# Two-layer hybrid decoder trunk: at the three layer ends, who normalises the first tokens, and where TensorE turns them

## The reference, cut to what matters

```
mod = (cs @ ada_w[l] + ada_b[l])[:, None, :]
sh_a, sc_a, g_a, sh_m, sc_m, g_m = jnp.split(mod, N_MOD, axis=-1)
x = layer_norm(DEEPNORM_ALPHA * x + (1.0 + g_a) * y, ln_g[l, 0], ln_b[l, 0])
h = x * (1.0 + sc_m) + sh_m
```

## Time and profile before

| what | value |
|---|---|
| median of three runs (lowest to highest) | 2274.39 us (2272.28 to 2275.78) |
| span of the profiled execution | 2271.9 us |
| TensorE busy | 2237.7 us, 98% |
| VectorE busy | 1722.1 us, 76% |
| ScalarE busy | 1142.2 us, 50% |
| mean granted TensorE clock | 0.998 of full |

### The profile page before, as it was taken

The page is one execution under the profiler, slowest core; times in us unless marked ns, Lnnn a source line. Parts: engine busy times, 40 slices in busy tenths (PEclk is TensorE's granted clock), DMA queues, the critical chain, the costliest instruction groups (busy, mean ns, idle before and its releaser), DMA issues.

```text
span 2271.9 us, 31928 instructions
## 1 busy us (share of the span) xinstructions
PE 2237.7 (98%) x10980; PEld 1882.2 (83%) x10980; DVE 1722.1 (76%) x1697; ACT 1142.2 (50%) x1420; POOL 19.0 (1%) x41
## 2 busy tenths in 40 slices
PE   7999999999999999999999999999999999999998
PEld 6887788788888888888888888888888888888886
DVE  6689788988888888898777867788766445556656
ACT  2144365565555554444555555555555555444443
POOL 1000000000000000000000000000000000000000
PEclk9999999999999999999999999999999999999999
DMA  9998899679999999969758766884877555755553
GB/s 393 417 371 328 343 390 385 219 287 370 378 372 378 374 371 347 342 241 356 284 218 324 271 237 233 317 311 135 310 286 264 188 187 201 255 192 193 194 206 127
DMA packets 146475, 658.61 MB, mean 290 GB/s; under 512 B 16496, under 2 KB 16816, under 8 KB 115792
## 3 DMA queue, kind: packets, MB, share of 16 engines
q1 hardware_dynamic: 144000, 642.05, 75.9%
q0 software_dynamic: 2384, 15.37, 1.7%
HBM read 655.22 MB, written 2.13 MB: 289 GB/s over the span
## 4 chain that ended last, share of the span: by engine, by line
PE 80%; DMA 9%; DVE 6%; issue 3%; ACT 2%; SPq 1%; DVEq 0%; ACTq 0%
PE ps L1421 19%; PE ps L1320 15%; PE ps L1324 15%; PE ps L1321 15%; PE ps L1425 10%; DMA mod_w<-in_mods 3%; DMA R<-in_mods 3%; DMA raw<-in_tiles 2%; DVE mod_w L880 2%; DVE w_lo L875 2%; ACT w_hi L436 1%; PE ps L1577 0%; PE ps L1523 0%; PE ps L1521 0%; PE ps L1522 0%
## 5 line engine op out<-in xcount | busy, mean ns | idle before, releaser
L875 DVE TENSOR_TENSOR w_lo<-raw,w_hi 128x1024 fp32r<-128x1024 f32 x720 | 877.4, 1223 | 451.1 <-ACT w_hi L436 447.2
L436 ACT ACTIVATE w_hi<-raw 128x1024 fp32r<-128x1024 f32 x720 | 760.3, 1059 | 837.0 <-PE ps L1324 374.9
L1320 PE MATMUL ps<-w_hi,h_both 128*128 128x512 f32 x1872 | 735.5, 393 | 2.3 <-ACT w_hi L436 2.3
L1321 PE MATMUL ps<-w_hi,h_both 128*128 128x512 f32 x1872 | 729.1, 389 | 0.0
L1324 PE MATMUL ps<-w_lo,h_both 128*128 128x512 f32 x1872 | 506.9, 390 | 2.8 <-DVE w_lo L875 2.6
L1421 PE MATMUL ps<-h_both,w_hi 128*128 128x512 f32 x1920 | 480.9, 392 | 0.0
L880 DVE SCALAR_TENSOR_TENSOR mod_w<-mod_w,cs 128x2048 f32<-128x2048 f32 x200 | 457.0, 2286 | 30.0 <-DMA mod_w<-in_mods 22.4
L1324 PEld LDWEIGHTS ps<-w_lo,h_both 128*128 128x128 f32 x1872 | 350.7, 188 | 79.7 <-DVE w_lo L875 6.6
L1320 PEld LDWEIGHTS ps<-w_hi,h_both 128*128 128x128 f32 x1872 | 351.6, 188 | 77.5 <-ACT w_hi L436 2.7
L1321 PEld LDWEIGHTS ps<-w_hi,h_both 128*128 128x128 f32 x1872 | 351.6, 188 | 72.3 <-issue 1.0
L1421 PEld LDWEIGHTS ps<-h_both,w_hi 128*128 128x128 f32 x1920 | 345.4, 189 | 61.8
(11 more groups left out here) (196 smaller groups left out, 1045.9 us busy)
## 6 DMA issues: line engine op xcount, KB each, us to landing
raw<-in_tiles SPq DMA_DIRECT2D x736, 512.0 KB, 4.8
mod_w<-in_mods SPq DMA_DIRECT2D x200, 1024.0 KB, 7.1
R<-in_mods SPq DMA_DIRECT2D x16, 1024.0 KB, 21.9
odd_raw<-in_tiles SPq DMA_DIRECT2D x16, 512.0 KB, 20.5
R<-in_tiles SPq DMA_DIRECT2D x16, 512.0 KB, 6.6
R<-in_ln_rows POOLq DMA_DIRECT2D x6, 1024.0 KB, 8.5
G<-in_mods SPq DMA_DIRECT2D x4, 1024.0 KB, 21.9
S<-in_mods SPq DMA_DIRECT2D x4, 1024.0 KB, 23.9
```

The lines of the kernel that those rows point to most:

```text
L436: nc.scalar.activation(w_hi[:, slot, :], raw[:, slot, :], ACT.Copy).then_inc(hi_ready, 1)
L875: nc.vector.tensor_tensor(w_lo[:, slot, :], raw[:, slot, :], w_hi[:, slot, :].bitcast(F32), ALU.subtract)\
L1320: mm(dst, h_hi[:, kt, toks], w_hi[:, slot, c], start=start, stop=False, skip_group_check=more)
L1321: return mm(dst, h_lo[:, kt, toks], w_hi[:, slot, c], start=False, stop=False, skip_group_check=more)
```

## The change

Three edits, at all three ends. **VectorE** now normalises columns 0 to 1023 of token group 0, with the instruction that L969 uses elsewhere, twice 512 columns. This stands inside the third part (token group 1, first block), between its multiply (L955) and its add (L956), and waits for the variance and for ScalarE's exponential. **ScalarE** loses the two tiny instructions and the two of 512 columns; the rest of its list, the quoted loop included, stays. **TensorE** loses the eight transposes of the identity, and makes the transposes of pairs 0 and 1 before the last of the 14 entries, not behind it; pairs 2 and 3 stay at the head of `early_tiles`.

```diff
-WARM = 8
             def layer_end(e, occ_n, occ, n_coef, co):
                 scale_of(occ_n, 0)
-                act.wait_ge(rstd_ready, 2 * occ_n + 1)
-                link(nc.scalar.activation(ssq[:, 0:1], rstd[:, 0:1], ACT.Copy, scale=-1.0))
-                link(nc.scalar.activation(ssq[:, 1:2], mv[:, 0, 0:1], ACT.Identity, scale=ssq[:, 0:1]))
-                for q in range(2):
-                    x = X[:, 0, q * SW:(q + 1) * SW]
-                    nc.scalar.activation(x, x, ACT.Identity, scale=rstd[:, 0:1], bias=ssq[:, 1:2]).then_inc(xn0_ready, 1)
                 act.wait_ge(coef_ready, n_coef)
...
-            def residual(occ, half, tok, alpha, ns=(0, 1), parts=LAST_PARTS):
+            def residual(occ, half, tok, alpha, ns=(0, 1), parts=LAST_PARTS, between=None):
...
                 link(nc.vector.tensor_tensor(stage, ps[:, bank:bank + len(ns), :].rearrange("p a n -> p (a n)"), G[:, cols], ALU.mult))
+                if between is not None:
+                    between()
                 link(nc.vector.scalar_tensor_tensor(X[:, tok, cols], X[:, tok, cols], alpha, stage, ALU.mult, ALU.add))
...
-            def last_parts(occ, alpha):
+            def last_parts(e, occ, alpha):
+                def first_columns():
+                    dve.wait_ge(var_ready, 2 * occ + 1)
+                    dve.wait_ge(rstd_ready, 2 * occ + 1)
+                    for q in range(2):
+                        x = X[:, 0, q * SW:(q + 1) * SW]
+                        nc.vector.tensor_scalar(x, x, mv[:, 0, 0:1], rstd[:, 0:1], ALU.subtract, ALU.mult).then_inc(xn0_ready, 1)
+
                 for tok, ns in LAST_PARTS:
-                    link(residual(occ, 1, tok, alpha, ns))
+                    link(residual(occ, 1, tok, alpha, ns, between=first_columns if (tok, ns) == LAST_PARTS[2] else None))
...
-                for pr in range(EARLY):
+                for pr in range(EARLY // 2, EARLY):
                     turn_token(occ, e, pr, 0)
...
-            def wide(t, half, first, src, hooks=None, last=False, down=False):
+            def wide(t, half, first, src, hooks=None, next_stage=None, down=False):
+                last = next_stage is not None
...
-                    for i in range(WARM):
-                        nc.tensor.transpose(ps[:, 1 if down else 5, (i % 4) * P:(i % 4 + 1) * P], ident[:], ident[:])
+                        if i == len(LAST_TILES) - 2:
+                            for pr in range(EARLY // 2):
+                                turn_token(*next_stage, pr, 0)
...
-            wide(O + 16, 1, True, narrow, last=True)
+            wide(O + 16, 1, True, narrow, next_stage=(H_M0, 0))
...
-                        wide(t + 3 * BODY, half, False, src(3), {}, last=True, down=True)
+                        wide(t + 3 * BODY, half, False, src(3), {}, next_stage=(H_Q, 1), down=True)
...
-            wide(O + 16, 1, True, heads, last=True)
+            wide(O + 16, 1, True, heads, next_stage=(H_M1, 2))
```

More of the change, by code:

```diff
@@ L986, in layer_end @@
             def layer_end(e, occ_n, alpha, occ, n_coef, co):
-                last_parts(occ_n, alpha)
+                last_parts(e, occ_n, alpha)
                 for q in range(2):
```

## The result

The changed kernel takes 2277.57 us (median of 21 runs, 2275.49 to 2281.78), the kernel before 2274.08 us (median of 21 runs, 2272.16 to 2276.31). The ratio is 1.0017, with a 95% interval of 1.0011 to 1.0022: slower by 3.5 us by the medians, inside the 0.2% that was called no change. 2276.7 was forecast. The span of the profiled execution is 2274.2 us against 2271.9, and the execution itself took 2275.9 us.

What follows compares the result with a forecast made beforehand. TensorE, busy 98% of the span, was taken as the bound, so longer layer ends reach the time in full. Delays of 0.74 + 0.79 + 0.78 = 2.31 us on 2274.39 gave 2276.7 us, range 2272.8 to 2280.0.

Steps and rivals of the forecast that it cites:

- TensorE busy in every microsecond between the ends: Windows behind the layer ends: TensorE never idle (682.00 of 682.00 us behind the first), so an end's delay counts in full.
- VectorE's add 1.02 us later: VectorE's third part at the first end: two normalisations push the add from 439.64 to 440.66, 1.02 us later.
- The release by the exponential: VectorE's third part: the normalisations start 0.11 us after ScalarE's exponential ends, at 439.73.
- the fourth part's slack: VectorE's fourth part: its waits for TensorE, 0.28, 0.23 and 0.24 us at the ends, absorb delay first.
- Idle transposes worth nothing: TensorE at each end: dropping eight idle transposes saves it 0.87 us, none of which reaches the time.
- the 1.33 us of head start: TensorE at the first end: with_hi can begin at 441.97 instead of 443.30, but none of this gain arrives.
- What is late next: ScalarE's pair 2 waits for token group 1's variance; TensorE stands still from 443.85 to about 445.9, two microseconds.
- The clock: At the layer ends, TensorE's clock falls in the two-microsecond stall: 1.7 us an end, 5.0 in all, 2281.7 us; 7%.

Runs made afterwards that it cites:

- vec_only: The changed kernel with TensorE's list of the kernel before (eight idle transposes kept, all four pairs turned behind the last entry); 2276.52 us, ratio 1.0009 to the kernel before.
- vec_double: The changed kernel with two more VectorE normalisations of 512 columns behind the new ones, into a free buffer nobody reads; 2281.56 us.
- no_idle: The kernel before without the eight idle transposes, nothing else changed; 2273.67 us, ratio 0.9999 to the kernel before.
- scale_late: The changed kernel with ScalarE's scale of token group 1 moved behind all four pairs' copies and the first h_lo copy; 2271.35 us, ratio 0.9994 to the kernel before.
- fill_transposes: The changed kernel with 16 identity transposes in TensorE's wait between the products of pairs 1 and 2; 2276.03 us.
- fill_products: The changed kernel with 8 unused products of 512 columns in TensorE's wait between the products of pairs 1 and 2; 2276.05 us.

## Why the prediction was right, and where it fell short

- **TensorE busy in every microsecond between the ends, so all of an end reaches the time:** it has no wait there after the change either. Held.
- **VectorE's add 1.02 us later:** measured 1.70 - 0.66 = 1.04. The release by the exponential took 0.14 us where 0.11 was taken.
- **Less the fourth part's slack, 0.74, 0.79 and 0.78 us for the ends, 2.31 in all:** the ends are 0.78, 0.80 and 0.78 longer, 2.36. vec_only gives the same length, and vec_double adds 0.92 for two more normalisations.
- **Idle transposes worth nothing, the 1.33 us of head start lost again:** no_idle changes an end by 0.03 us; the head start was 1.50 less 0.15 by which the entries came earlier, 1.35, and all of it went into the wait.
- **What is late next:** ScalarE's pair 2 behind the scale of token group 1, TensorE idle for two microseconds. It is 1.9 us, three times. scale_late removes it by that order alone.
- **The clock:** here the text fell short. It weighed the fall as a case of its own, at 7%, that either takes the ends or not, and its reason against it was that the kernel before has only transposes and a short wait from 441.09 to 443.30 at a clock of 1.00. The reason was sound for a stretch with transposes in it, as fill_transposes shows, and was carried over to one without. In truth the fall comes in some executions, at one end or another, about half of the runs having a mean clock that speaks for one. The price was near: 1.7 us a fall was taken, 1.48 measured (1.3 and 1.1 in vec_double). So the mechanism was right for 2.4 of the 3.5 us. The other 1.1 us were in no term of the sum. The clock, set to nothing there, should have had one; that it makes up the whole 1.1 is an estimate from medians and not shown.

## What to carry to other kernels

Ask for each wait in an engine's list what is queued behind it that does not need it: here the scale of the second half's tokens stood in front of copies that were ready, and moving that one call was worth more (1.5 us an end) than all the work that the change took off TensorE and ScalarE. Work that is taken off the busiest engine brings nothing where another chain ends last, and an engine's slack (0.28 us ahead of the fourth part) is used up before a cost shows, so read it first. And where TensorE is left idle for about two microseconds between products, count the chance of a slower clock behind it too, and look at more than one profile for it.

## What the runs showed that was not expected

- The same kernel, with the same wait of 1.9 us, has its clock at 1.00 behind it in five of the six ends that were profiled, and a mean of 0.57 over the next window in one. With 2.8 us it fell in two of three.
- The fall at the program's start, which gave the prediction its price, is not bound to the first long wait either: in fill_products' profile TensorE waited 3.87 us up to 16.07 and the clock was 1.00 from 16 to 20 us; it fell later, behind a wait of 2.10 us that ended at 44.64 (0.61 from 44 to 48 us).
- Filling the wait by transposes of the identity kept the clock up as well as products did: no run of 11 at 0.996 with either. The eight idle transposes of the kernel before took 0.87 us at each end and cost nothing, since they stood in front of a wait.
